# HGRN2's first decays in layer 0 moved from block step 8 to block step 7

## What is computed

```
proj = x @ w_in;  hq, hf, hi, hg, ... , su = split(proj)
f_gate = lb + (1 - lb) * sigmoid(hf)           # decay of each channel and token
k_hg   = (1 - lb) * sigmoid(-hf)
S_t = diag(f_t) S_{t-1} + k_t v_t^T,   o_t = S_t^T q_t,   q = silu(hq), v = hi
# retention: the same with a fixed decay; S5: a complex diagonal recurrence on su
x = layer_norm(ALPHA * x + mixed @ w_out)
x = layer_norm(ALPHA * x + relu(x @ w_up)^2 @ w_down)
```

## Time and profile before

| | |
|---|---|
| median of 3 runs | 871.01 us (870.61 to 872.6) |
| the profiled execution: its own time | 873.37 us |
| its span, first to last instruction | 871.6 us |
| mean granted TensorE clock, share of full speed | 0.927 |
| PE busy | 765.7 us, 88% |
| DVE busy | 551.7 us, 63% |
| ACT busy | 387.2 us, 44% |

### The profile page before, as it was taken

One profiled execution on the slowest core, in us unless ns is written; L12 is line 12 of the kernel. 1 busy time (PEld: TensorE's weight loads), 2 busy tenths in 40 slices (PEclk: granted clock), 3 DMA queues, 4 the chain that ended last, 5 costly groups with the idle time before them and its releaser, 6 DMA issues. The chain is left out here.

```text
span 871.6 us, 18223 instructions
## 1 busy us (share of the span) xinstructions
PE 765.7 (88%) x7662; PEld 722.5 (83%) x7662; DVE 551.7 (63%) x974; ACT 387.2 (44%) x672; POOL 36.1 (4%) x44
## 2 busy tenths in 40 slices
PE   4759668989799978999997989799897999999994
PEld 3759657878699878999996988698786999999993
DVE  7996994344566699764446789734556665466543
ACT  4726132453475522456327525343436553355423
POOL 4000010300000000000000002010000000000000
PEclk9979886997979999999997999899797999999998
DMA  8432111342234534653541323312241555554521
GB/s 333 148 122 74 51 50 54 139 158 97 97 107 163 166 110 140 204 176 123 183 166 55 106 99 100 137 59 97 72 145 57 184 172 193 180 183 170 192 99 50
DMA packets 30577, 113.59 MB, mean 130 GB/s; under 512 B 3520, under 2 KB 3728, under 8 KB 29984
## 3 DMA queue, kind: packets, MB, share of 16 engines
q1 hardware_dynamic: 27936, 101.83, 35.0%
q0 software_dynamic: 1984, 9.52, 2.9%
q10 hardware_dynamic: 576, 1.08, 0.3%
HBM read 108.24 MB, written 4.18 MB: 129 GB/s over the span
## 5 line engine op out<-in xcount | busy, mean ns | idle before, releaser
L1301 DVE TENSOR_TENSOR w_low<-w_raw,w_high 128x1024 fp32r<-128x1024 f32 x192 | 236.7, 1233 | 203.3 <-ACT w_high L957 201.4
L912 PE MATMUL stream<-a_high,w_high 128*128 128x264 f32 x1024 | 317.5, 310 | 41.3 <-DVE a_low L1306 31.1
L957 ACT ACTIVATE w_high<-w_raw 128x1024 fp32r<-128x1024 f32 x192 | 202.1, 1054 | 289.9 <-PE stream L914 265.1
L913 PE MATMUL stream<-a_low,w_high 128*128 128x264 f32 x1024 | 305.3, 298 | 0.0
L914 PE MATMUL stream<-a_high,w_low 128*128 128x264 f32 x1024 | 304.5, 297 | 0.0
L912 PEld LDWEIGHTS stream<-a_high,w_high 128*128 128x128 f32 x1024 | 207.9, 203 | 55.0 <-issue 29.9
L913 PEld LDWEIGHTS stream<-a_low,w_high 128*128 128x128 f32 x1024 | 208.7, 204 | 0.4
L914 PEld LDWEIGHTS stream<-a_high,w_low 128*128 128x128 f32 x1024 | 207.5, 203 | 0.0
L912 PE MATMUL stream<-h_high,w_high 128*128 128x264 f32 x512 | 150.0, 293 | 10.3 <-DVE w_low L1301 8.1
L913 PE MATMUL stream<-h_low,w_high 128*128 128x264 f32 x512 | 145.8, 285 | 0.0
L914 PE MATMUL stream<-h_high,w_low 128*128 128x264 f32 x512 | 145.6, 284 | 0.0
(11 more groups left out here) (331 smaller groups left out, 739.9 us busy)
## 6 DMA issues: line engine op xcount, KB each, us to landing
w_raw<-in_weights SPq DMA_DIRECT2D x192, 512.0 KB, 3.3
mats<-in_matrices POOLq DMA_DIRECT2D x2, 1024.0 KB, 5.3
S_hg<-in_state_hg POOLq DMA_DIRECT2D x2, 768.0 KB, 4.7
out_hg_s<-S_hg POOLq DMA_DIRECT2D x2, 768.0 KB, 3.7
consts<-in_constants POOLq DMA_DIRECT2D x1, 1484.5 KB, 9.1
X<-in_xT ACTq DMA_DIRECT2D x4, 264.0 KB, 5.8
out_y<-X SPq DMA_DIRECT2D x1, 1056.0 KB, 3.9
S_rt<-in_state_rt POOLq DMA_DIRECT2D x2, 512.0 KB, 6.3
```

Source lines behind the costliest of these rows:

```text
L912: pe.matmul(bnk[:, 0:T], wh, xh, start=(first and kk == 0), stop=False)
L913: pe.matmul(bnk[:, 0:T], wh, xl, start=False, stop=False)
L957: act.activation(w_high[:, n % SPLIT_SLOTS, :], w_raw[:, n % RAW_SLOTS, :], ACT.Copy).then_inc(high_ready, 1)
L1301: put(tt(w_low[:, n % SPLIT_SLOTS, :], w_raw[:, n % RAW_SLOTS, :], w_high[:, n % SPLIT_SLOTS, :].bitcast(F32), ALU.subtract), low_ready)
```

## The change

In layer 0, `c == 6 + s` is c = 8, and `c == FIRST_LEVEL[l] - 2` is c = 7. In layer 1 both are c = 6. So in layer 0 DVE's `level_decay(0, 0)` with its wait for the cleared buffers, and ACT's two copies with their waits, stand one block step earlier in their queues. Nothing is added or removed, and PE's plan, POOL and SP are untouched.

```diff
@@ -1049,7 +1049,7 @@
                 elif HGT < c <= HGT + 5:
                     gate_sigmoid(l, c - 1 - HGT)
                 s = LATER[l]
-                if c == 6 + s:
+                if c == FIRST_LEVEL[l] - 2:
                     act.wait_ge(gate_ready, 9 * l + 9)
                     act.wait_ge(cleared, 5 + l)
                     k2 = Kg[:, :, 0:256].rearrange("p f (n c) -> p f n c", c=2)
```

## The result

The changed kernel takes 864.11 us, median of five runs (863.78 to 864.68), against 871.25 (870.61 to 872.6) before: ratio 0.9911, 95% interval 0.9897 to 0.9925, so 7.1 us less. Counted over all executions that the experiments brought with them, the kernel before has a mean of 871.6 (130 executions, 868.1 to 874.8) and the changed one 864.8 (24 executions, 863.1 to 869.5): 6.9 us. One more execution of the kernel before, in a slow state of the chip (1043.8 us at a mean granted clock of 0.667), is left out.

The account below looks back on a forecast made before the run. DVE was taken to bound the stretch up to its tables, PE behind them. The table units end at 67.7 instead of 72.25, 4.5 us less: 868.9 from the profiled 873.37, 866.5 from the median; range 865.0 to 869.3.

Parts of the forecast that it names:

- the gain stops at the tables and the banks: PE's table units: 6.9 us gained by block 10 shrinks to 4.5, as tables stay at 64.57 and banks free at 66.5.
- The term of 4.5 us: Gain at the end of PE's last table unit in layer 0: 72.25 now, 67.7 after the change.
- a pause of 1.5 us: PE's pause between block 8 and level 0's first part, foretold to shrink from 5.74 to about 1.5 us.
- another of 0.92: Unexplained pause of 0.92 us in PE's block 9, which may stay or go; the sum kept it.
- PE's slack ahead of the tables: PE has about 2 us of waiting to give, mostly hiding a clock fall before block 9 or 10.
- Does it last?: Step behind the table units: PE is the bound, everything on it comes 4.5 us earlier, DVE's cover is 3.5 us.
- rival 3: Slower: from 93.2 to 176 us pauses fall so that half clock lasts longer; 875.6 us; chance 0.05.
- I cost them at nothing: Later loads, POOL's work and the second layer, all released by the same chain, were priced at zero.
- How the numbers follow: Section giving the chances: forecast 0.55, faster by over 1.7 us 0.85, within that 0.10, slower 0.05.
- a gain above 6 us: Last case, whole kernel: fewer half-clock stretches further on give more than 6 us; chance 0.10.
- Rival 1: Clock falls behind the last pause, ahead of block 11: takes 2.5 us, leaves 2.0, giving 869.0; chance 0.20.
- The rule on transposes: Transposes do not hold the clock up as matmuls do, so 63.4 to 67.7 counts as one long pause.

Follow-up runs that it names:

- act_only: Kernel before with only ACT's two copies moved to block step 7, DVE's decays staying at step 8: median 871.78 us, ratio 0.9999.
- near_early: Changed kernel with layer 0's masked copy of level 0 at the end of DVE's block step 9 instead of in step 10: median 868.36 us.
- b_warm8: Kernel before plus 42 idle matmuls on PE ahead of the first part of level 0 in layer 0: median 869.01 us, ratio 0.9967.
- dve_only: Kernel before with only DVE's decays moved to block step 7, ACT's two copies staying at step 8: median 866.07 us, ratio 0.9942.
- a_fourth: Changed kernel repeated unchanged, for its fourth trace: median 864.03 us over 6 executions, traced execution 864.41 us.
- a_wait: Changed kernel with PE's level 0 in layer 0 also waiting for query tile 2: median 872.70 us, ratio 1.0008.
- before: First trace of the kernel before, nothing altered; that execution took 873.37 us.
- b_again: Kernel before repeated unchanged, for a second trace: median 872.78 us over 10 executions, traced execution 873.21 us.
- b_third: Kernel before repeated unchanged, for a third trace: median 871.42 us over 12 executions, traced execution 872.88 us.
- b_shift: Kernel before plus 9 matmuls (1.1 us) on PE ahead of block 11 in layer 0: median 871.1 us, mean 872.1 us.
- b_warm8b: Repeat of the kernel before with 42 idle matmuls ahead of level 0 in layer 0: median 867.52 us, ratio 0.9954.

## Why the prediction was wrong, point by point

**Right.** That DVE is the bound up to the tables and PE behind them; that L1533 was what PE waited for, though the trace names no one; that ACT's copies cost nothing (`act_only`); that the gain stops at the tables and the banks, not at the pause; and the starts on DVE and at the tables: L1533, the tables' end, the last unit, the copy of level 1 at 77.0. The term of 4.5 us was 4.6 in the first trace, 3.4 to 4.6 in four. PE's way to the tables was not right: a pause of 1.5 us missing, another of 0.92 grown to 1.52, and block 8 slow. These errors came to 0.9 us at the end of block 10, and that they did not show is owed to PE's slack ahead of the tables, which the prediction had named.

**The step that failed** is "Does it last?": "everything on it comes 4.5 us earlier". So it is in `near_early` (4.6 at the last block), and the local gain of `b_warm8` also lasts (2.9, and 2.6 at the last block). In the four traces of the changed kernel and in that of `dve_only` the way from level 1 to the end is 2.0 to 5.6 us shorter than in the first trace of before, mostly between blocks 17 and 36, in most of them again near block 122. I had this as rival 3 with its sign turned, at 0.10, and it was the case that came. The changed kernel took 786.3 to 789.8 us behind level 1, the kernel before 791.7 to 791.8. In the sum this is the term put at nothing ("I cost them at nothing"): it came to 4.6 us in the first pair of traces and to about 2.5 in the medians. In "How the numbers follow" it stood as "a gain above 6 us", which begins at 865.0 (871.0 - 6), just where the range ends.

**What misled.** I took the runs of before, within 2 us of each other, for a sign that the clock's scatter is small. 130 executions scatter by 6.7 us. The profile had said more: a mean clock of 0.84 from 93 to 176, with 26 us at half, and a PE that is busy for four fifths of it. That is a term of the sum for any change that moves what lies ahead of it, in either direction, and the range should have held 3 us more below.

**Rival 1** happened in `a_fourth`, at 1.2 us instead of 2.5: the fall came ahead of the tables, where PE has waiting to give, not behind them. The rule on transposes that the prediction quotes from the Trainium skill ("TensorE: Matmul & The Clock Gate", Part 4: PE-mode transpose) was not borne out in this trace: behind the first table units the clock stayed at 1.00 in the changed kernel (58.40 to 91.00), with its waits of 0.36 and 0.88 us.

**What stays open** is what ties a fall of the clock to its place, and why the changed kernel so often gets the favourable place: 17 of 24 executions lie within 1.6 us of its fastest, 21 of 130 of the kernel before. That the fallen clock ties the kernel before to a poor place has this for it: `a_wait`, with the pause back, is mostly in a poor place again (2 of 12, though its trace took 789.3), and in the four traces with the old order and nothing added (`before`, `b_again`, `b_third`, `act_only`) the changes of clock lie up to 0.9 us apart while level 1 moves by 0.5 only, so it partly moves with them. Against it: `b_shift`, whose mean did not fall; `b_warm8` and `b_warm8b`, without the fallen clock, are near their fastest in only 7 of 24, and `near_early` in 4 of 12. These counts are small. That the distant part goes through the pause is shown by `a_wait`; by what way from there, isn't settled.

## What to carry to other kernels

When one engine is full and another sleeps for it, reorder the full one's queue by who waits for what: here 1.7 us of work moved ahead of a split that nobody needed yet took 4.5 us off, and the sum made from starts and durations met DVE's starts and the last table unit within 0.1 us. Price a pause of TensorE not by its length alone but also by the clock behind it, which was here the larger part (some 2.8 of 4.6 us). And where a long stretch alternates between pauses and half clock, a small shift ahead of it may be worth more than the change itself: take many executions, and compare traces whose clock falls alike.

## What the runs showed of the hardware

What the clock costs depends on where its falls lie in the work, and goes in jumps: with the same work and order the stretch behind level 1 took 786 to 792 us, and 787.6 and 791.4 in two traces whose first fall lay 0.1 us apart. Falls come at other places in other executions of the same kernel: block 8 ran at full clock in one and at half in the next, behind the same work. A pause of 5.75 us filled with idle matmuls gave 2.9 us by the end of the table units in one trace, and 3.7 by the copy of level 1 in another. But 45 to 58 us less at half clock, bought by filling twelve pauses, gave about 6 us on the kernel before and nothing certain on the changed one.
